# Short identity matmuls in the waits of TensorE during the residual norms of a transformer step

## The reference

```python
x = x + ga1 * rmsnorm(mix_x, g_post_mix[i])
fx = rmsnorm(x, g_pre_ffn[i]) * (1.0 + sc2) + sh2
yx = conv_ffn(fx, w_up[i], w_ffn_conv[i], b_ffn_conv[i], w_down[i])
x = x + ga2 * rmsnorm(yx, g_post_ffn[i])
```

## Time and profile before

| | |
|---|---|
| Median of 3 runs | 2337.94 us (2337.73 to 2342.42) |
| Profiled execution | 2337.68 us, span 2335.9 us |
| Busy in the span | TensorE 2174.0 us (93%), VectorE 1470.7, ScalarE 1036.1, GpSimd 696.1 |
| Mean granted clock of TensorE | 0.961 |
| Chain that ended last, by engine | TensorE 69%, VectorE 16%, ScalarE 4%, GpSimd 2% |
| L859, L868, L888, L846 (recorded instructions) | 256, 40, 46, 104 |

### The profile page before, as it was taken

One profiled execution on the slowest core, in us unless ns is written; L12 is line 12 of the kernel. 1 busy time (PEld: TensorE's weight loads), 2 busy tenths in 40 slices (PEclk: granted clock), 3 DMA queues, 4 the chain that ended last, 5 costly groups with the idle time before them and its releaser, 6 DMA issues.

```text
span 2335.9 us, 31442 instructions
## 1 busy us (share of the span) xinstructions
PE 2174.0 (93%) x11670; PEld 1732.6 (74%) x11670; DVE 1470.7 (63%) x2654; ACT 1036.1 (44%) x1566; POOL 696.1 (30%) x316
## 2 busy tenths in 40 slices
PE   4999999799998999988999989999989998989997
PEld 2777658588887888875666768888877866777776
DVE  3575854478866688666677455435433258289998
ACT  3423852342322233215357254334333258368775
POOL 1231002422223223222410344444454424223223
PEclk8999999799999999987999979999999999999999
DMA  7431022223333233231310112222222223369997
GB/s 262 154 107 48 37 71 88 73 73 109 122 109 114 73 119 122 98 108 67 125 47 37 46 54 97 96 98 99 98 82 83 96 75 74 120 260 396 345 349 262
DMA packets 81757, 285.69 MB, mean 122 GB/s; under 512 B 10665, under 2 KB 13130, under 8 KB 80780
## 3 DMA queue, kind: packets, MB, share of 16 engines
q1 hardware_dynamic: 74768, 259.26, 31.7%
q0 software_dynamic: 3168, 13.68, 1.5%
q10 hardware_dynamic: 3676, 10.84, 1.3%
HBM read 277.96 MB, written 9.48 MB: 123 GB/s over the span
## 4 chain that ended last, share of the span: by engine, by line
PE 69%; DVE 16%; ACT 4%; issue 3%; DMA 3%; POOL 2%; DVEq 2%; SPq 1%; ACTq 0%
PE ps L766 31%; PE ps L835 11%; DVE mlo L2785 4%; PE ps L811 4%; DVE ps L2490 4%; PE ps L1513 3%; PE ps L1121 2%; PE ps L1137 2%; PE ps L1373 2%; PE ps L1070 2%; PE ps L1531 2%; DMA wraw<-in_w_all 2%; POOL x L677 1%; PE ps L1178 1%; PE ps L896 1%
## 5 line engine op out<-in xcount | busy, mean ns | idle before, releaser
L671 POOL TENSOR_TENSOR wlo<-wraw,whi 128x1024 fp32r<-128x1024 f32 x208 | 504.7, 2429 | 1084.9 <-ACT whi L1561 637.2
L766 PE MATMUL ps<-hhi,whi 128*128 128x512 f32 (+1 forms) x1568 | 570.0, 364 | 5.5 <-POOL wlo L671 4.5
L766 PE MATMUL ps<-hlo,whi 128*128 128x512 f32 (+1 forms) x1568 | 563.8, 360 | 0.0
L766 PE MATMUL ps<-hhi,wlo 128*128 128x512 f32 (+1 forms) x1568 | 560.8, 358 | 0.0
L766 PEld LDWEIGHTS ps<-hhi,whi 128*128 128x128 f32 x1568 | 295.9, 189 | 73.9 <-issue 22.6
L766 PEld LDWEIGHTS ps<-hhi,wlo 128*128 128x128 f32 x1568 | 295.1, 188 | 46.1
L766 PEld LDWEIGHTS ps<-hlo,whi 128*128 128x128 f32 x1568 | 295.7, 189 | 43.8 <-issue 1.0
L1561 ACT ACTIVATE whi<-wraw 128x1024 fp32r<-128x1024 f32 x132 | 139.1, 1055 | 307.2 <-DMA wraw<-in_w_all 229.7
L2490 DVE CUSTOM_DVE_ANT_0 ps<-wraw,crow,mod 128x256 f32<-128x256 f32 x384 | 223.6, 643 | 16.7 <-issue 10.3
L2785 DVE TENSOR_TENSOR mlo<-mraw,mhi 128x1024 fp32r<-128x1024 f32 x147 | 207.7, 1443 | 4.6 <-ACT mhi L2024 4.5
L835 PE MATMUL ps<-ahi,whi 128*128 128x512 f32 (+1 forms) x528 | 187.6, 355 | 0.5 <-POOL wlo L671 0.4
(11 more groups left out here) (375 smaller groups left out, 3809.1 us busy)
## 6 DMA issues: line engine op xcount, KB each, us to landing
wraw<-in_w_all SPq DMA_DIRECT2D x288, 512.0 KB, 3.5
mraw<-in_w_moe SPq DMA_DIRECT2D x168, 512.0 KB, 6.1
mraw_b<-in_w_mod SPq DMA_DIRECT2D x10, 512.0 KB, 15.4
slot_rows<-in_slot_rows ACTq DMA_DIRECT2D x1, 3612.0 KB, 18.1
xs<-slot_rows POOLq DMA_DIRECT2D x7, 516.0 KB, 7.2
mraw_a<-in_w_mod SPq DMA_DIRECT2D x6, 512.0 KB, 10.8
x<-in_xT SPq DMA_DIRECT2D x1, 2048.0 KB, 9.9
fl<-in_four ACTq DMA_DIRECT2D x2, 1024.0 KB, 5.7
```

The lines of the kernel that those rows point to most:

```text
L671: pool.tensor_tensor(wlo[:, slot, :], wraw[:, AT_W[n] % RING, :], whi[:, slot, :].bitcast(F32), ALU.subtract).then_inc(lo_split, 1)
L766: m = pe.matmul(ps[:, bank + b, 0:w], a, r[:, c0:c0 + w], start=k == 0 and q == 0, stop=k == KT - 1 and q == 2)
```

## The change

A new helper `keep_warm(count, bank)` issues `count` float32 matmuls of the identity by the identity, 128 columns each. They wait for no semaphore and signal none. They write the second bank of the two-bank tile that the next stream of large matmuls opens with (bank 3 or 5); nothing reads it before that tile starts over it. The calls go only into TensorE's program:

```diff
+        def keep_warm(count, bank):
+            for _ in range(count):
+                pe.matmul(ps[:, bank, 0:P], ident[:, :], ident[:, :], start=True, stop=True)
+
-        def squares(key, width):
+        def squares(key, width, idle):
+            keep_warm(17, idle)
             for k in range(KT):
                 square(key, width, k, 2)
+                keep_warm(6 if k < KT - 1 else 2, idle)
             turn_squares(key, width)
+            keep_warm(5, idle)
...
             if L:
-                squares((L, "premix"), T)
+                squares((L, "premix"), T, bank2(T0) + 1)
                 spread((L, "premix"), T)
+                keep_warm(18, bank2(T0) + 1)
...
+            idle = bank2(T0 + IN_T + OUT_T) + 1
             summed_squares((L, "postmix"), W, mix_nth(L))
+            keep_warm(5, idle)
             spread((L, "postmix"), W)
-            squares((L, "preffn"), W)
+            squares((L, "preffn"), W, idle)
             spread((L, "preffn"), W)
+            keep_warm(18, idle)
...
             summed_squares((L, "postffn"), W, ffn_nth(L) + CHUNKS - 1)
+            keep_warm(5, bank2(T0 + LAYER_TILES) + 1)
             spread((L, "postffn"), W)
+            if L:
+                keep_warm(17, bank2(B2_TILE) + 1)
```

## The result

The changed kernel is slower: 2345.09 us against 2341.40, medians of 20 runs each, ratio of the runs 1.0022, 95% interval [1.0013, 1.0031] (the two medians alone are 3.7 us apart). By the ratio that is about 5 us (3 to 7) of 2341. The forecast was +6 us, 2343.8, in a range of 2336 to 2351.

A forecast was written before the change was run, and what follows sets the result against it. TensorE, busy in 93% of the span, was taken as the bound nearly everywhere. A +0.9, B +2.1, C +4.7 and D -1.3 sum to +6.4 us, rounded to +6 on 2337.68: 2343.8 us, range 2336 to 2351.

The forecast's parts named there:

- A: Norm pair of width T, half clock in the profile before: 0 + 4.1 - 1.5 - 1.7 = +0.9 us.
- The squares' step: Start-to-start time of squares behind six fillers: 2.0 us at T, 1.8 at TX; +4.1 at A and B, +5.75 at C.
- upper bounds of +5.1, +5.1 and +6.9: Most the squares could cost at A, B and C, with 0.24 and 0.1 us for each change of weights.
- What the clock gave back: Gains at full clock: second spread at T -1.5 us, turn at B -1.1, `first_tiles` at A -1.7, at C -1.3 before fillers.
- B: Norm pair of width T, half clock for 33.9 us: 0.7 + 0.3 + 4.1 - 0.4 - 1.1 - 1.5 = +2.1 us.
- C: Norm pair of width TX: squares +5.75 us the largest term, sum +4.7.
- D: Last of the four places, half clock for 10.0 us: 0.2 - 1.5 = -1.3 us.
- first spread and its fillers: First spread and the 5 fillers ahead: A 0, B +0.7, C -0.1, D +0.2 us; bounds +1.0 to -1.5 at T.
- The sum: All four places: A +0.9, B +2.1, C +4.7, D -1.3, together +6.4 us, rounded to +6.
- cheap-filler rival: Clock stays up, fillers at low price, squares' step about 1.5 us at T: -3 us, 2335; chance 0.17.
- The third: Rival: fillers don't raise the clock, squares' step 3.5 us at T, 3.2 at TX: +79 us, 2417; chance 0.07.
- estimate from the Trainium skill: Four 56 ns passes, 0.223 us a filler: 126 fillers between squares cost 1.5 us less, sum +4.5.

The follow-up runs named there:

- e6: Changed kernel with 3 fillers in place of 6 behind each of the first seven squares; ratio 0.9964 to the kernel before.
- e2: Changed kernel with fillers sized to each wait: behind the squares, and at C also 12 for 17, 13 for 18; ratio 0.9958 to the kernel before.
- e1: Changed kernel without the six fillers behind each of the first seven squares, all others kept; ratio 0.9992 to the kernel before.
- e9: The same program as e2, measured again beside other runs on one chip; ratio 0.9952 to the kernel before.
- e5: e2 plus fillers in the waits ahead of the one-column sums, 18 at B and 6 at D; ratio 0.9946 to the kernel before.
- e3: Changed kernel with every filler cut to one moving column, identity weights still loaded in full; ratio 1.0303 to the kernel before, +71 us.
- e4: Changed kernel with only the six fillers behind each of the first seven squares, all others left out; ratio 1.0088 to the kernel before, +21 us.
- e11: e2 with 2 fillers for 5 ahead of each first spread, plus nine float32 matmuls at the program's start; ratio 0.9967 to the kernel before.
- e12: e11 plus 6 fillers in the 1.6 us wait ahead of D's one-column sums; ratio 0.9957 to the kernel before.
- e10: e2 with 2 fillers for 5 ahead of each first spread, no matmuls added at the start, a repeat run; ratio 0.9991 to the kernel before.

## Why the prediction held, and which terms were off

**The mechanism.** Right: the fillers between the squares turned TensorE into the bound of the squares. As foretold, POOL was done with its additions at A at 450.5, 7.8 us before the last square, and ACT waited for L868. e6 and e2 against the changed kernel show it, each by the numbers between the squares and the waits they stand in. e1 adds what I had not seen, that with none the clock falls there.

**The squares' step.** 2.10 us at T and 1.89 at TX, against 2.0 and 1.8 predicted. Six fillers took 1.53, not 1.41 and a little; the term was mis-sized by 5%. Its two parts were both off. The chain of e2 at A has groups of different size between squares:

```profile
442.17 1.31 PE ps L854 x10
...
447.81 0.42 PE ps L854 x2
...
448.80 1.09 PE ps L854 x8
```

Four more fillers take 0.89 us, 0.222 each, less than the 0.235 of L1051, and 0.20 is left in every group for the two changes of weights, where the prediction had 0.04 a change and 0.1 as its bound. The step cost 4.8, 4.8 and 13.24 - 6.85 = 6.4 us, 16.0 for the 14.0 forecast. (The upper bounds of +5.1, +5.1 and +6.9 add to +3.2 over the forecast, not to the +4.3 in the prediction's sum.)

**What the clock gave back.** Second spread at A 1.58 for 2.94: -1.4 for -1.5. Turn at B 1.36 to the next matmul in the chain, 1.50 in the timeline, for 2.72: -1.2 for -1.1. `first_tiles` at A 17.71 for 19.51: -1.8 for -1.7. At C 10.93 for 12.53, -1.6 for -1.3, less the fillers ahead: 18 took 4.02 against a wait of 3.15.

**The sites.** A +1.7 for +0.9; B +2.0 for +2.1; C +3.6 for +4.7; D +0.4 for -1.3. At A the larger squares' term is most of the error. At C the clock did not fall at all, not even in the first spread (0.98 for 2.08), a bound that I had named but not taken. D was the one wrong sign in this trace. The term that was off there is the one for the first spread and its fillers, taken as +0.2: the sums ran at half (+0.9), the 5 fillers took 2.34 us against a wait of 1.1 (+1.2), and the spread gave back only 0.4; the -1.5 of `first_tiles` did come. In part this is chance. D has the same fillers in e1, e2, e6 and e9; it took 26.2 and 26.2 us where the clock fell some 1 us after the start of the sums, as here, and 24.9 and 25.0 where it fell 2 us or more after it, which is near the -1.3 forecast. In every one of these traces a wait of 1.6 us stood ahead of the sums, as in the kernel before; the prediction noted the 4.4 us ahead of the sums at B and passed over this one. In e5, which fills it, the clock did not fall at D at all.

**The sum.** +7.7 us at the places of one execution for +6.4; the timed 5 us (3 to 7) is nearer to the forecast. The rest of the spans' difference, 2.9 us, is in stretches without a filler; what differs there is not shown.

**The rivals.** The cheap-filler rival fell by the step of 2.10, against its 1.5. The third was excluded for this filler and realised by e3. The rule on program order that the prediction took from the Trainium skill (TensorE: Matmul & The Clock Gate, "The mechanism" of Part 3) agrees with the rows: no square passed a filler in any trace, and where the squares' `nsq` came early, in e4 and the changed kernel, they stood behind L854. The estimate from the Trainium skill (TensorE: Matmul & The Clock Gate, "Back-to-back issue gap", with the four passes of FP8 and Floating Point Precision, "TensorE Precision Notes"), 0.223 us a filler, agrees with the 0.222 that each further filler took here; what it leaves out is the 0.20 us of the two changes of weights, with which six fillers came to 1.53. (Its +4.5 in the prediction is counted from the rounded +6; from +6.4 it is +4.9.)

## What to carry to other kernels

Filler matmuls can win back TensorE's clock in a chain that it waits on (here 0.4 to 0.5% when sized), but each must fit the wait in front of the next real instruction, measured at the full clock and step by step: the first three steps between squares were 1.78 us long, the later ones 0.85 to 1.64. When a filler is oversized, halve it before dropping it; three held the clock as well as six, none did not. And look at what else ends near the wait: at B VectorE held the spread as soon as the sums were faster, and the clock fell in the new wait.

## What the runs showed of the hardware

- TensorE busy for 50.00 of 50.00 us stayed at 1.2 GHz where most of its matmuls moved one column (e3, at A), and at C the clock fell from 2.4 GHz without an idle moment in the profile; the same count with 128 columns ran at 2.4 GHz.
- At 2.4 GHz a float32 matmul of 128 columns with its weight load took 0.222 us behind its like; the change to a square's 32-column weights and back cost 0.20 us more (e2).
- Nine fewer matmuls ahead of a loop brought a stall of 2.9 to 3.1 us for issue behind the loop's first matmul and nine more instruction packets, in both traces of that program; nine added at the start removed it, in both traces that have them (e11, e12). That the stall hangs on where the code lies, and not on the count of fillers in the loop, is what e11 shows; what exactly comes late was not tried. e10 against e11 is 0.24%, as much as the change under study, and the stall explains about half of that.
- Where the granted clock dips outside the norms differs between executions of the same program: B's end to C's start took 255.6 us in e2 and 257.9 in e9, which are one program (258.6 before). Single traces of this kernel don't tell apart less than some 3 us.
